# The mixer's output product split by input half, and the constants table loaded in two pieces

## The reference, cut to what matters

```python
m   = silu(cond) @ w_ada[0] + b_ada[0]                 # 6 pieces of 1024 per sequence: the modulation
a   = modulate(rms_norm(h), m[0], m[1])
z   = a @ w_in                                         # recurrent (rwkv) part and state-space (mamba) part
y_rw, y_mb = rwkv7_scan(...), ssd_chunked(...)         # both directions, 8 heads of 64 each
o_rw = (group_norm(y_rw) * rw_gn_w + rw_gn_b + bonus) * gate
y_mb = rms_norm((y_mb + d * x) * silu(zg)) * mb_norm_w
h   = h + m[2] * (concat([o_rw, y_mb]) @ w_out)        # "mix out": K = 1024, the first 512 rows of w_out
                                                       # meet o_rw, the last 512 meet y_mb
h   = h + m[5] * swiglu(modulate(rms_norm(h), m[3], m[4]))
```

## Time and profile before

| | us |
|---|---|
| median of 3 runs | 3348.21 (3347.99 to 3348.7) |
| the profiled execution, its time | 3348.48 |
| its span, first to last instruction | 3346.7 |
| PE busy in the span | 3127.8 (93%) |
| VectorE busy | 1319.6 (39%) |
| ScalarE busy | 525.2 (16%) |
| mean granted TensorE clock | 0.963 of full speed |

### The profile page before, as it was taken

One profiled execution on the slowest core, in us unless ns is written; L12 is line 12 of the kernel. 1 busy time (PEld: TensorE's weight loads), 2 busy tenths in 40 slices (PEclk: granted clock), 3 DMA queues, 4 the chain that ended last, 5 costly groups with the idle time before them and its releaser, 6 DMA issues.

```text
span 3346.7 us, 52452 instructions
## 1 busy us (share of the span) xinstructions
PE 3127.8 (93%) x22488; PEld 2078.3 (62%) x22488; DVE 1319.6 (39%) x2980; ACT 525.2 (16%) x1170; POOL 0.2 (0%) x4
## 2 busy tenths in 40 slices
PE   7999899997999997989999999999998879998998
PEld 5454799996344432457865554455557568876887
DVE  1468666665399986721420010001002232112211
ACT  2114222222100000012421100101112120012000
POOL 0000000000000000000000000000000000000000
PEclk8999999998999998999989999999999889999999
DMA  6241001001377784431079999999975113541352
GB/s 247 87 151 50 1 1 39 1 1 52 114 237 233 235 254 146 159 129 51 1 297 346 337 340 345 364 364 355 339 245 164 59 51 126 151 126 51 126 151 63
DMA packets 351450, 551.14 MB, mean 165 GB/s; under 512 B 14496, under 2 KB 292256, under 8 KB 347904
## 3 DMA queue, kind: packets, MB, share of 16 engines
q1 hardware_dynamic: 351232, 547.89, 49.2%
HBM read 546.80 MB, written 1.05 MB: 164 GB/s over the span
## 4 chain that ended last, share of the span: by engine, by line
PE 85%; DVE 10%; ACT 2%; DMA 1%; issue 1%; SPq 0%; DVEq 0%; ACTq 0%
PE bank L653 17%; PE bank L1304 14%; PE bank L914 9%; PE bank L1326 8%; PE bank L1484 7%; PE bank L1095 5%; DVE mix L2030 4%; PE bank L1111 4%; PE bank L617 3%; PE bank L732 3%; PE bank L1138 2%; PE bank L898 1%; PE bank L1249 1%; DMA ring<-in_w_ada 1%; PE bank L1393 1%
## 5 line engine op out<-in xcount | busy, mean ns | idle before, releaser
L653 PE MATMUL bank<-a,ring 128*128 128x256 f32 (+1 forms) x1792 | 454.4, 417 | 22.2 <-ACT a L1581 11.8
L653 PEld LDWEIGHTS bank<-a,ring 128*128 128x128 f32 x1792 | 346.3, 194 | 127.9 <-issue 74.7
L1304 PE MATMUL bank<-ring,arena 128*32 128x352 f32 x5376 | 407.1, 461 | 2.0 <-ACT small L1825 2.0
L2030 DVE SCALAR_TENSOR_TENSOR mix<-arena,csil,mix 128x256 f32<-128x256 f32 x1008 | 405.4, 482 | 0.1
L1095 PE MATMUL bank<-a,ring 128*128 128x512 f32 x704 | 307.8, 597 | 6.8 <-ACT a L1581 6.8
L1304 PEld LDWEIGHTS bank<-ring,arena 128*32 128x32 f32 x5376 | 177.6, 110 | 218.2 <-issue 201.4
L1095 PEld LDWEIGHTS bank<-a,ring 128*128 128x128 f32 x704 | 133.6, 191 | 180.3 <-issue 178.3
L1484 PE MATMUL bank<-arena,ring 128*128 128x256 f32 x1024 | 223.5, 379 | 2.0 <-DVE arena L2684 2.0
L2586 DVE TENSOR_TENSOR arena<-arena,bank 128x352 f32<-128x352 f32 x48 | 25.0, 521 | 501.4 <-ACT arena L1838 501.4
L1585 ACT ACTIVATE arena<-bank 128x256 f32<-128x256 f32 (+1 forms) x303 | 141.8, 473 | 491.1 <-PE bank L914 198.4
L1326 PE MATMUL bank<-ring,arena 128*32 128x256 f32 (+1 forms) x3840 | 218.6, 380 | 0.0
(11 more groups left out here) (409 smaller groups left out, 3325.3 us busy)
## 6 DMA issues: line engine op xcount, KB each, us to landing
ring<-in_moe_w SPq DMA_DIRECT2D x224, 704.0 KB, 8.5
ring<-in_mlp_w SPq DMA_DIRECT2D x64, 1024.0 KB, 5.5
ring<-in_moe_w SPq DMA_DIRECT2D x112, 512.0 KB, 8.5
arena<-in_ada_w SPq DMA_DIRECT2D x96, 512.0 KB, 3.6
arena<-in_w_ada SPq DMA_DIRECT2D x48, 512.0 KB, 3.6
ring<-in_ffn_w SPq DMA_DIRECT2D x22, 1024.0 KB, 7.2
arena<-in_moe_w SPq DMA_DIRECT2D x32, 704.0 KB, 8.9
ring<-in_moe_w SPq DMA_DIRECT2D x48, 384.0 KB, 8.5
```

Source lines behind the costliest of these rows:

```text
L653: i = mm(bank[b][:, 0:n], ws[:, k, t * P:t * P + P], src, start=(k == 0), stop=(k == KT - 1))
L1304: i = mm(b[32 * t:32 * t + 32, 0:PART], ac_[:, k, 32 * g:32 * g + 32], ws[i_][:, PART * t:PART * t + PART], start=(k == 0), stop=(k == KT ...
L2030: ins = V.scalar_tensor_tensor(dst, x, cond, dst, ALU.mult, ALU.add)
```

## The change

The program's only new instructions are a few waits and one DMA. It does the following.

1. **Constants.** At the start only the columns 0 to 255 (`ident` and `mean`) are loaded. The other 4228 columns come under a semaphore of their own, `more_in`, together with `rows`, `mu_g` and the router's weights, just before the ring's load of slot s = 3 (the first of xbc's), so behind the slots 0 to 2. PE waits for `more_in` before the sums called cs, VectorE before the masks of the gram matrices.
2. **Mix out.** `mix_part(j, ks)` multiplies output tile j by the K tiles `ks`. For j = 0 to 4 the half k = 4 to 7 (from `ym_t`) is put ahead of the wait for "yr norm", each tile in a bank of its own (1, 2, 3, 4, 7). The turning uses the banks 5 and 6 in turn, with a wait for "gn" j - 2. Then each tile gets its half k = 0 to 3, where tile 0 waits for ("o_rw", k) piece by piece; the tiles 5 to 7 have both halves there.
3. **Reload.** The second load of the inputs into `hT` is issued after ("y", 15), the last mark of the scan, not after "o_rw". The chunks and the ring stay behind "o_rw" and ("yr turned", 3).

```diff
+EARLY = CO["head"]
+MIX_BANKS = (1, 2, 3, 4, 7)
@@ SP
-            sy.dma_start(consts, w["consts"]).then_inc(consts_in, 16)
+            sy.dma_start(consts[:, 0:EARLY], w["consts"][:, 0:EARLY]).then_inc(consts_in, 16)
             for k in range(KT):
                 sy.dma_start(ada_first[k], ada_src[:, k, 0:ADA_COLS]).then_inc(ada_in[k], 16)
-            sy.dma_start(rows, w["rows"]).then_inc(loaded, 16)
-            sy.dma_start(mug[0:96, :], w["mu_g"]).then_inc(loaded, 16)
-            sy.dma_start(router_w, w["moe_router_w"][0].rearrange("(k p) n -> p k n", p=P)
-                         ).then_inc(router_in, 16)
...
+                if s == 3:
+                    sy.dma_start(rows, w["rows"]).then_inc(loaded, 16)
+                    sy.dma_start(mug[0:96, :], w["mu_g"]).then_inc(loaded, 16)
+                    sy.dma_start(consts[:, EARLY:NCONST], w["consts"][:, EARLY:NCONST]).then_inc(more_in, 16)
+                    sy.dma_start(router_w, w["moe_router_w"][0].rearrange("(k p) n -> p k n", p=P)
+                                 ).then_inc(router_in, 16)
...
                 if s == first["ffn"]:
-                    sy.wait_ge(vec_done, at(VE, "o_rw"))
-                    sy.wait_ge(pe_done, at(PE, ("yr turned", 3)))
-
+                    sy.wait_ge(pe_done, at(PE, ("y", 15)))
                     for sl, name in ((CTX, "ctxT"), (LAT, "xT")):
                         sy.dma_start(hT[:, :, sl], w[name].rearrange("(k p) n -> p k n", p=P)
                                      ).then_inc(again_in, 16)
+                    sy.wait_ge(vec_done, at(VE, "o_rw"))
+                    sy.wait_ge(pe_done, at(PE, ("yr turned", 3)))
@@ PE
+            pe.wait_ge(more_in, 16)
             pe.wait_ge(vec_done, at(VE, "a_tok"))
...
+            def mix_part(j, ks):
+
+                sl = first["mix_out"] + j // 2
+                ws = full(sl)
+                for k in ks:
+                    src = mix[:, k, :] if k < 4 else ym_t[:, k - 4, :]
+                    if j == 0 and k < 4:
+                        pe.wait_ge(vec_done, at(VE, "o_rw" if k == 3 else ("o_rw", k)))
+                    i = mm(bank[MIX_BANKS[j % 5]], ws[:, k, j % 2 * P:j % 2 * P + P], src,
+                           start=(k == 4), stop=(k == 3), skip_group_check=True)
+                if ks[-1] == 3:
+                    i.then_inc(pe_done, did(PE, ("mix out", j), *([("slot", sl)] if j % 2 else [])))
+
+            for j in range(5):
+                mix_part(j, (4, 5, 6, 7))
             pe.wait_ge(vec_done, at(VE, "yr norm"))
             for j in range(4):
-                turned(("yr turned", j), lambda m: yt[:, m, j * P:j * P + P], 1 + j)
-            pe.wait_ge(vec_done, at(VE, "o_rw"))
-            product("mix out", first["mix_out"], 4, mix, slice(0, T), [6, 7],
-                    lambda j: pe.wait_ge(vec_done, at(VE, ("mix res", j))), more=ym_t,
-                    then=lambda j: square_in(1, slice(0, T), j))
+                if j >= 2:
+                    pe.wait_ge(act_done, at(AC, ("gn", j - 2)))
+                turned(("yr turned", j), lambda m: yt[:, m, j * P:j * P + P], 5 + j % 2)
+            for j in range(KT):
+                if j >= 5:
+                    pe.wait_ge(vec_done, at(VE, ("mix res", j - 5)))
+                    mix_part(j, (4, 5, 6, 7))
+                mix_part(j, (0, 1, 2, 3))
+                if j:
+                    square_in(1, slice(0, T), j - 1)
+            square_in(1, slice(0, T), KT - 1)
@@ ACT
-                act(mix[:, j, :], bank[1 + j], ACT.Identity, scale=col("rw_gn_w", j),
+                act(mix[:, j, :], bank[5 + j % 2], ACT.Identity, scale=col("rw_gn_w", j),
@@ DVE
             V.tensor_copy(small[:, 192:256], bank[6][:, 0:64]).then_inc(vec_done, did(VE, "cs"))
+            ve.wait_ge(more_in, 16)
             ve.wait_ge(pe_done, at(PE, "gram"))
...
-                residual("mix res", j, bank[6 + j % 2], (0, 0, 2), (0, 1))
+                residual("mix res", j, bank[MIX_BANKS[j % 5]], (0, 0, 2), (0, 1))
```

More of the change, by code:

```diff
@@ L289, in build @@
         cols_in, h_in, consts_in, loaded = (sem(n) for n in ("cols_in", "h_in", "consts_in", "loaded"))
+        more_in = sem("more_in")
         ada_in = [sem(f"ada_in{k}") for k in range(KT)]
@@ L637, in normed, with product @@
                 pe.wait_ge(act_done, at(AC, ("norm", st, k, 1)))
-            def product(name, s0, n_slots, rhs, sl, banks, before, of=None, then=None, more=None):
+            def product(name, s0, n_slots, rhs, sl, banks, before, of=None, then=None):
                 n = sl.stop - sl.start
@@ L651, in product @@
                                 normed(of, k)
-                            src = rhs[:, k, sl] if more is None or k < 4 else more[:, k - 4, sl]
-                            i = mm(bank[b][:, 0:n], ws[:, k, t * P:t * P + P], src,
+                            i = mm(bank[b][:, 0:n], ws[:, k, t * P:t * P + P], rhs[:, k, sl],
                                    start=(k == 0), stop=(k == KT - 1))
```

## The result

| | median, us | range | runs |
|---|---|---|---|
| before | 3348.45 | 3347.99 to 3352.48 | 4 |
| after | 3323.62 | 3319.90 to 3324.87 | 4 |

The ratio is 0.9925, with a 95% interval of 0.9910 to 0.9941: faster by 0.75%, against a forecast median of 3324.0. The profiled execution of the changed kernel took 3324.87 us with a span of 3323.0, 23.7 less than the span of before.

A forecast was written before the change was run, and what follows sets the result against it. It took the `w_ada` transfer to bound the start, and PE's 13.4 us idle behind the scan plus a cold clock to cost the middle. 5.2 + 19.0 = 24.2 off 3348.48 gave 3324.3, median 3324.0; range 3320 to 3331.

The forecast's parts named there:

- The start: At the head of the DMA queue: 2114 KB of constants moved from ahead of `w_ada` save 5.2 us.
- the 45 to 57 of the forecast: Near the start: VectorE's wait for `rows` and `mu_g` stands until some 45 to 57 us, at no cost.
- The estimate for the 128 KB left in front: Constants still loaded first: as a small transfer 0.6 to 0.9 us, where bytes at the trace's rate give 0.3.
- 1 us for each change of the clock: Later in the program: each clock change can fall some 1 us earlier or later, within a likeliest 3321 to 3328.
- The middle: From the scan to the last mix-out tile: the product ends at 869.9 instead of 888.94, a gain of 19.0 us.
- the units moved: Mix-out product: 20 units of 0.86 us run on PE ahead of the turning, a gain of 17.2 us.
- the three units under VectorE: First mix-out tile: k = 0 to 2 run while VectorE finishes the remaining gated tiles, a gain of 2.6 us.
- the late turning: After the group norm: the early halves end at 822.05, so the turning starts later, a cost of 3.8 us.
- The cold clock's 3.0: First two mix-out tiles: they took 16.80 us from a start at clock 0.50; the change regains 3.0 us.
- The rival of a clock that falls between the late pieces: From 822 to 830 us: clock drops to 0.50 in PE's gaps, 3.0 us come back, 3327.0; chance 0.09.
- The reload at nothing: Second load of the inputs, issued at the scan's end: lands at 814.5 and slows VectorE's passes by nothing.
- The rest: After mix-out: the VectorE-bound next stage moves whole with its start, so both gains, 5.2 and 19.0 us, reach the end.

The follow-up runs named there:

- warm_filler: The kernel before with 15 useless matmuls on PE between the scan and the turning, no mix-out work moved: 3347.98 us against a base of 3348.32.
- whole_wait: The changed kernel with the first mix-out tile waiting for all four gated tiles at once, not each: scan to last tile 70.23 us, median 3328.27.
- before_again: The kernel before, unchanged, run once more for its trace: 3349.23 us in one run, scan to last tile 84.11.
- after_again: The changed kernel, unchanged, run once more: 3324.67 us against a base of 3347.8, scan to last tile 64.66.

## Why the prediction was right

**The start.** Forecast 5.2 us from bytes ahead of `w_ada`; measured 4.91. Over all profiles the eighth ada step starts at 35.11 to 35.56 in the four kernels with the constants in front and at 30.04 to 30.31 in the ten without, 5.1 us apart in the mean. The step held, as did its checks: the norm was ready 4.8 us early (forecast 5.7; PE's squares began at 10.67 and took 9.92 us, not 9.06), the ring's loads and the late constants made nobody wait, and VectorE had its small tables at 37.4, before the 45 to 57 of the forecast. The estimate for the 128 KB left in front, 0.6 to 0.9 us, was too high for this place in a queue: they landed at 2.26 + 8.0 = 10.26, 0.4 us behind the inputs, and PE's first matmul, at 10.67, waits for ScalarE's first square and not for them.

**What I hadn't in the sum.** The start's gain isn't carried to the scan at 4.9 but with the clock's luck in dt, xbc and behind, 2.8 in the first pair of profiles (6.4 in the mean of all), so that the last tile ends 22.2 us earlier and not 24.2. I allowed 1 us for each change of the clock; the length of dt and xbc alone spreads over 3.3 us in executions of one program.

**The middle.** Forecast 19.0, measured 19.4 (84.09 - 64.66). Of the terms, the units moved (17.2), the three units under VectorE (2.6) and the late turning (3.8) came as worked out. The turning, at the full clock, gave 0.7 more: from its start to the last gated tile it takes 6.76 instead of 7.44 us; 0.3 went again where the five units at 826.08 take 4.56 instead of 4.3. The cold clock's 3.0 came too, but by my account it belonged to PE being busy through the norm. There the size was right and the reason wrong: PE was busy through the norm in warm_filler too, which gained nothing, and in whole_wait, which loses the 3.0 us by leaving out the three lone units. The rival of a clock that falls between the late pieces had been priced at 3.0 and given 0.09: that is what happens when these units are taken away.

**The reload at nothing.** Held: VectorE's pass under the transfer takes 2.29 us, as before. And the price of leaving it in place, a first sum held up, was measured at 7.1.

**The rest.** From the last tile to the end of the span it takes 2456.3 us, before 2457.8 (2456.3 and 2456.4 in the changed kernel's other profiles, 2457.6 in before_again). VectorE was full there as before, 104.97 of 105 us at 1040. The gain was not absorbed; the 1.5 us more lie mostly in the feed-forward stage (0.9 up to the attention's first product), whose start had a shorter stretch at 0.50. That this is the cause was not tried.

**The sum.** 4.9 - 2.1 (clock) + 19.4 + 1.5 = 23.7, that of the spans; the forecast was 24.2. That it came so near is partly luck: the clock between the start and the scan took 2.1 us, the middle and the rest gave 1.9 more than forecast, and another pair of executions has another sum (the scan's end alone moved by 8.2 us in before and after_again).

## What to carry to other kernels

Where a serial stretch of one engine stands between two products, look for the half of the next product whose operands are ready, and fill exactly that stretch: a piece beyond it delays the in-order queue by its own length and gains nothing. Split the wait at the stretch's end by piece; here it saved more than the pieces' own time (5.6 us, of which 2.6 were theirs), because it also kept TensorE's clock up. And after shortening the first tile, look at what was covered by its length: here a transfer that had to move with it.

## What the hardware showed that I hadn't expected

The clock fell while the profile shows PE busy without a gap: at 72 to 84 us of the changed kernel's first profile it stood at 0.50 with 4.00 of 4.00 us busy, during and behind 64 instructions of 128x16. The same instructions in groups of 16 between products of 128x512 ran at 1.00 and cost 6.8 us. A busy share of 100% in the profile doesn't say that the clock holds; the clock's own column does.
